# First attention beside the late projections, second beside the scan's second half and half of the output projection, with two w_in buffers

## What is computed

```python
proj = rmsnorm(x, norm1_g[l]) @ w_in[l]
pa, pb, pc, pd = jnp.split(proj, cut, axis=-1)
out_a = moba_attention(qa, ka, va, ...)      # attention "A", 4 heads of 64
out_b = rwkv7_time_mix(pb, ...)              # the scan, two channel halves c = 0, 1
out_c = sgu_mix(uc, vc, ...)                 # gated position mixing
out_d = diff_attention(qd, kd, vd, ...)      # attention "D", two softmaxes per head
mixed = jnp.concatenate([out_a, out_b, out_c, out_d], axis=-1)
x = x + mixed @ w_out[l]
x = x + hier_moe(rmsnorm(x, norm2_g[l]), ...)
```

## Time and profile before

| | us |
|---|---|
| median of 3 runs | 2249.1 |
| lowest and highest | 2246.83, 2253.64 |
| the profiled execution | 2240.36 |
| its span, first to last instruction | 2238.7 |

### The profile page before, as it was taken

One profiled execution on the slowest core, in us unless ns is written; L12 is line 12 of the kernel. 1 busy time (PEld: TensorE's weight loads), 2 busy tenths in 40 slices (PEclk: granted clock), 3 DMA queues, 4 the chain that ended last, 5 costly groups with the idle time before them and its releaser, 6 DMA issues. The chain is left out here.

```text
span 2238.7 us, 23731 instructions
## 1 busy us (share of the span) xinstructions
PE 1760.2 (79%) x9640; PEld 1014.2 (45%) x9640; DVE 583.6 (26%) x1175; ACT 328.0 (15%) x663; POOL 112.5 (5%) x133
## 2 busy tenths in 40 slices
PE   6799987698977768878379999777988877776862
PEld 3356574244544434444134656533544444443430
DVE  1262533543111111111124425334421111111113
ACT  1211233311000000000012121333100000000001
POOL 0010000001000000000100000000010000000001
PEclk9899996599998999889789999856999989998986
DMA  8911110025999999999541110100379999999993
GB/s 285 272 47 38 38 38 1 0 85 197 365 412 414 415 413 412 415 412 407 185 185 48 52 52 1 38 0 1 120 274 413 413 415 412 413 415 413 412 365 127
DMA packets 107426, 527.16 MB, mean 235 GB/s; under 512 B 35044, under 2 KB 35812, under 8 KB 88420
## 3 DMA queue, kind: packets, MB, share of 16 engines
q1 hardware_dynamic: 64740, 476.28, 52.6%
q0 software_dynamic: 38400, 33.79, 4.7%
q10 hardware_dynamic: 4224, 16.25, 3.0%
HBM read 482.03 MB, written 44.04 MB: 235 GB/s over the span
## 5 line engine op out<-in xcount | busy, mean ns | idle before, releaser
L747 PE MATMUL banks<-RING,TOK 128*64 128x256 f32 x4224 | 482.9, 384 | 75.4 <-DMA RING<-in_w_up 39.0
L747 PEld LDWEIGHTS banks<-RING,TOK 128*64 128x64 f32 x4224 | 322.0, 138 | 252.8 <-DMA RING<-in_w_up 52.6
L762 PE MATMUL banks<-RING,XS 128*64 128x512 f32 x1056 | 278.0, 673 | 39.7 <-issue 27.0
L463 PE MATMUL banks<-RING,XNT 128*128 128x512 f32 x512 | 238.5, 603 | 0.0
L762 PEld LDWEIGHTS banks<-RING,XS 128*64 128x64 f32 x1056 | 90.9, 156 | 187.8 <-issue 186.2
L1003 ACT ACTIVATE XS<-banks 128x256 f32<-128x256 f32 x64 | 24.6, 384 | 987.8 <-PE banks L747 987.8
L1374 DVE TENSOR_TENSOR XS<-XS,banks 128x256 f32<-128x256 f32 x66 | 27.8, 421 | 494.2 <-PE banks L747 494.2
L740 PE MATMUL banks<-CF,TOK 128*128 128x128 f32 (+1 forms) x272 | 53.5, 360 | 112.0 <-DMA TOK<-x_slots 109.9
L463 PEld LDWEIGHTS banks<-RING,XNT 128*128 128x128 f32 x512 | 92.2, 192 | 90.8 <-issue 90.4
L454 PE MATMUL banks<-XNT,RING 128*128 128x512 f32 x256 | 110.4, 593 | 2.8 <-DMA RING<-in_w_in_blocks 1.6
L1395 DVE COPY XS<-banks 128x512 f32<-128x512 f32 x64 | 44.3, 692 | 252.9 <-PE banks L762 252.9
(11 more groups left out here) (257 smaller groups left out, 1698.1 us busy)
## 6 DMA issues: line engine op xcount, KB each, us to landing
RING<-in_w_gate SPq DMA_DIRECT2D x66, 2048.0 KB, 27.3
RING<-in_w_up SPq DMA_DIRECT2D x66, 2048.0 KB, 28.1
RING<-in_w_down SPq DMA_DIRECT2D x66, 2048.0 KB, 25.3
RING<-in_w_in_blocks SPq DMA_DIRECT2D x12, 2048.0 KB, 11.7
TOK<-x_slots SPq DMA_DIRECT2D x32, 512.0 KB, 23.5
y_slots<-XS POOLq DMA_DIRECT2D x64, 256.0 KB, 19.2
x_slots<-TOK ACTq DMA_DIRECT2D x11, 1024.0 KB, 30.6
RING<-in_w_out_blocks SPq DMA_DIRECT2D x4, 2048.0 KB, 7.6
```

Source lines behind the costliest of these rows:

```text
L463: last = mm(bank[:, :], XNT[:, k, i * P:(i + 1) * P], w[:, k, :], start=(k == 0), stop=(k == KD - 1))
L747: last = mm(bank[f * CAP:(f + 1) * CAP, 0:256], XT[:, k, h * CAP:(h + 1) * CAP], w[:, k, f * 256:(f + 1) * 256], start=(k == 0), stop=(k = ...
L762: last = mm(PS[5][n * CAP:(n + 1) * CAP, :], HT[:, j, f * CAP:(f + 1) * CAP], w[:, k, n * BN:(n + 1) * BN], start=(k == 0), stop=(k == KF ...
```

## The change

- `SLOT` buffers for `w_in`: two instead of three, so that the third is free for A's and D's turned queries and keys (`QKT`) and probabilities (`PB`). The load of expert 0's gate weights moves from the end of the projections to the end of the mixers, since it goes to that buffer.
- The late projections share one PSUM bank (2) instead of two; the scan uses banks 1, 3 and 4.
- M and E steps are cut in two (q = 0, 1), so a scan half has 45 steps.
- All of scan half 0 and all of attention A are put beside the late projections; all of scan half 1 is put beside attention D, by the table `SCAN_PER_PART` (three scan steps behind each of D's first nine parts, two behind five, one behind eight).
- Half of the output projection (the inputs from A and from the gated mixer, k = 0, 1, 4, 5) is done during D in eight pieces of four matmuls (`out_half`), each added to X by VectorE in that order (`add_half`); the other half follows D.
- The gated mixer is done in two pieces, and group t(3,2) waits for the first, t(3,3) for the second; its two transposes (`turn_gated`) stand between the last projection and D.

```diff
+SCAN_PER_PART = [3] * 9 + [2] * 5 + [1] * 8
+SCAN_BANKS = (1, 3, 4)
...
-        QKT = view(XNTb, 0, 2048, "p (j t) -> p j t", j=4)
-        PB = view(XNTb, 2048, 2048, "p (b m t) -> p b m t", b=2, m=2)
         SLOT = [RING[:, s * 4096:(s + 1) * 4096] for s in range(6)]
+        QKT = view(RING, 2 * 4096, 2048, "p (j t) -> p j t", j=4)
+        PB = view(RING, 2 * 4096 + 2048, 2048, "p (b m t) -> p b m t", b=2, m=2)
...
-        MT = view(SC, 2048, 1024, "p (j t) -> p j t", j=2)
+        MT = view(XNTb, 0, 1024, "p (j t) -> p j t", j=2)
...
-        bank_of = [g % 8 if g < LATE else (0, 5)[g % 2] for g in range(len(PROJ))]
+        bank_of = [g % 8 if g < LATE else 2 for g in range(len(PROJ))]
...
-            steps = ([("P", q) for q in range(4)] + ["T"] + [(part, n) for n in range(1, 7) for part in "ME"]
+            steps = ([("P", q) for q in range(4)] + ["T"] + [(part, n, q) for n in range(1, 7) for q in range(2) for part in "ME"]
                      + [(part, ch) for ch in range(4) for part in "ZBS"] + [("F", n) for n in range(3)] + ["G"])
-            scan = [(c, m, step) for c, m in ((0, "A"), (1, "D")) for step in steps]
-            scan.remove((0, "A", "G"))
-            for g in range(LATE, len(PROJ)):
+            scan = {c: [(c, m, step) for step in steps] for c, m in ((0, "A"), (1, "D"))}
+            scan[0].remove((0, "A", "G"))
+            parts = {m: [(m, u, part) for u in range(PAIRS + n) for part in range(2)] for m, n in (("A", 2), ("D", 3))}
+
+            def late(g, quarter, steps):
+                yield "proj", (g, quarter)
+                for _ in range(steps):
+                    yield "rwkv", scan[0].pop(0)
+                if quarter == 3 and PROJ[g] == ("t", (2, NT - 1)):
+                    yield "sgu_in", ()
+                if quarter == 3 and PROJ[g] in (("t", (3, 1)), ("t", (3, 2))):
+                    yield "sgu_out", (PROJ[g][1][1] - 1,)
+
+            attended = PROJ.index(("t", (2, 0)))
+            for g in range(LATE, attended):
                 for quarter in range(4):
-                    yield "proj", (g, quarter)
-                    for _ in range(1 if g > LATE else (0, 0, 0, 4)[quarter]):
-                        yield "rwkv", scan.pop(0)
-                if PROJ[g] == ("t", (2, NT - 1)):
-                    yield "sgu_in", ()
-                if PROJ[g] == ("t", (3, 1)):
-                    yield "sgu_out", ()
-            for m, u in [("A", u) for u in range(PAIRS + 2)] + [("D", u) for u in range(PAIRS + 3)]:
-                yield "attn", (m, u, 0)
-                if scan:
-                    yield "rwkv", scan.pop(0)
-                else:
-                    yield "out", (u - PAIRS + 1,)
-                yield "attn", (m, u, 1)
-                if m == "A" and 1 <= u <= 4:
-                    yield "rwkv", scan.pop(0)
+                    yield from late(g, quarter, 1 if g > LATE else 0)
+            for n in range(4 * (len(PROJ) - attended)):
+                yield from late(attended + n // 4, n % 4, 2 if n % 8 == 7 else 1)
+                if n % 3 < 2 and parts["A"]:
+                    yield "attn", parts["A"].pop(0)
+            for t in range(2):
+                yield "sgu_turn", (t,)
+            for n, steps in enumerate(SCAN_PER_PART):
+                yield "attn", parts["D"].pop(0)
+                for _ in range(steps):
+                    yield "rwkv", scan[1].pop(0)
+                if n >= 6 and n % 2 == 0:
+                    yield "out", divmod((n - 6) // 2, NT)
+            assert not any(scan.values()) and not any(parts.values())
...
-                        if n >= 3:
-                            sp.wait_ge(proj_ps, BLOCK_USED[n - 3])
-                        sp.dma_start(SLOT[n % 3], w_in[one, n].rearrange("a p n -> p (a n)")).then_inc(slot_full[n % 3], 16)
+                        if n >= 2:
+                            sp.wait_ge(proj_ps, BLOCK_USED[n - 2])
+                        sp.dma_start(SLOT[n % 2], w_in[one, n].rearrange("a p n -> p (a n)")).then_inc(slot_full[n % 2], 16)
...
-                        sp.wait_ge(proj_ps, BLOCK_USED[n + 3])
+                        sp.wait_ge(proj_ps, BLOCK_USED[n + 4])
...
-                    load(0, 0, [(proj_ps, BLOCK_USED[5]), (mixed_done, 1), (mixed_done, 1)])
+                    load(0, 0, [(mixed_done, 1), (mixed_done, 1), (mixed_done, 1)])
...
+                            if PROJ[g] in (("t", (3, 2)), ("t", (3, 3))):
+                                pe.wait_ge(sgu_done, PROJ[g][1][1] - 1)
...
+                            _, n, q = step
+                            if n == 1:
+                                pe.wait_ge(s["turned"], 3)
+                                pe.wait_ge(s["eye"], 6)
+                            else:
+                                pe.wait_ge(s["de_merged"], 4 * (n - 2) + 2 * q + 2)
+                            if n > 1 or q:
+                                pe.wait_ge(s["m1_copied"], 2 * (n - 1) + q)
+                            for w in range(4):
+                                u = 4 * q + w
+                                last = mm(PS[1][:, w * P:(w + 1) * P], UB[:, u, 0:P], DB[:, u, :], start=True, stop=True)
+                            last.then_inc(s["m1_ps"], 1)
...
+                    def turn_gated(t):
+                        if t == 0:
+                            pe.wait_ge(sgu_done, 2)
+                            pe.wait_ge(proj_copied, len(PROJ) - 8)
+                        else:
+                            pe.wait_ge(mt_a, 1)
+                        for i in range(NT):
+                            last = tr(PS[2][:, i * P:(i + 1) * P], UV[:, i, t * P:(t + 1) * P], ident)
+                        last.then_inc(mt_ps, 1)
...
+                            pe.wait_ge(proj_copied, copied("t", (1, NT - 1)) if m == "A" else len(PROJ) - 8)
...
+                    def out_half(n, i):
+                        if n + i == 0:
+                            pe.wait_ge(mt_a, 2)
+                            pe.wait_ge(mix["A"]["o_done"], 2)
+                        else:
+                            pe.wait_ge(res_added, 4 * n + i)
                         if i == 0:
-                            pe.wait_ge(slot_full[0], 48)
-                            pe.wait_ge(mt_a, 2)
-                            pe.wait_ge(mix["D"]["y_done"], 1)
-                        project_out(0, i, range(KD - 2))
-
-                    run_mixers(proj=project, rwkv=rwkv, attn=attn, sgu_out=mix_positions, out=out_but_last)
+                            pe.wait_ge(slot_full[n], 64)
+                        project_out(n, i, (0, 1, 4, 5), 2).then_inc(res_ps, 1)
+
+                    run_mixers(proj=project, rwkv=rwkv, attn=attn, sgu_out=mix_positions, sgu_turn=turn_gated, out=out_half)
...
+                    pe.wait_ge(mix["D"]["y_done"], 1)
+                    pe.wait_ge(res_added, 8)
+                    for i in range(NT):
+                        project_out(0, i, (2, 3), OUT_BANK[i], last=False)
                     pe.wait_ge(sub_done, 2)
                     for i in range(NT):
-                        project_out(0, i, (KD - 2, KD - 1))
-                    pe.wait_ge(slot_full[1], 48)
+                        project_out(0, i, (6, 7), OUT_BANK[i], first=False).then_inc(res_ps, 1)
                     for i in range(NT):
-                        project_out(1, i, range(KD))
+                        project_out(1, i, (2, 3, 6, 7), OUT_BANK[NT + i]).then_inc(res_ps, 1)
...
+                    def add_half(n, i):
+                        dve.wait_ge(res_ps, 4 * n + i + 1)
+                        xv = X3[:, i, n * BN:(n + 1) * BN]
+                        V.tensor_tensor(xv, PS[2][:, :], xv, ALU.add).then_inc(res_added, 1)
+
+                    run_mixers(rwkv=rwkv, attn=attn, sgu_in=norm_v, sgu_out=gate_u, out=add_half)
```

More of the change, by code:

```diff
@@ new lines, in rwkv @@
+                            last.then_inc(s["m1_ps"], 1)
+                        elif step[0] == "E":
+                            _, n, q = step
+                            pe.wait_ge(s["m1_copied"], 2 * (n - 1) + q + 1)
+                            for side in range(2):
+                                if n == 6 and side == 0:
+                                    continue
+                                if n == 6:
+                                    pe.wait_ge(s["de_merged"], 20 + q)
+                                elif n > 1 or q > 0:
+                                    pe.wait_ge(s["de_merged"], 4 * (n - 1) + 2 * q + side - 1)
@@ L563, in rwkv @@
+                                    if side == 0:
+                                        last = mm(PS[3][:, w * P:(w + 1) * P], EB[:, u, :], MB[:, u, :], start=True, stop=True)
+                                    else:
+                                        last = mm(PS[4][:, w * P:(w + 1) * P], MB[:, u, :], EB[:, u, :], start=True, stop=True)
+                                last.then_inc(s["de_ps"], 1)
                         elif step[0] == "Z":
@@ L764, in down @@
```

(10 more changed lines are left out.)

142 lines of the change are left out of this document (51 added, 91 removed).

## The result

| | us |
|---|---|
| before, median | 2248.0 |
| changed, median of 4 runs | 2323.6 |
| lowest and highest of the changed kernel | 2319.4, 2329.4 |
| ratio, with its 95% interval | 1.034 (1.030 to 1.038) |
| profiled execution of the changed kernel, and its span | 2326.4, 2324.7 |

The change makes the kernel slower by 75.6 us. 2300 was predicted, with a range of 2238 to 2355. The two profiled executions stand 86.0 us apart, which is what the traces have to account for.

What follows compares the result with a forecast made beforehand. TensorE was taken to bound the late projections, with idle and clock loss elsewhere. Idle 92.3 plus clock 25 less 89.8 gave +27.5 us in layer 0, +29.2 in layer 1, less 5: 2249 + 52, rounded to 2300 us, range 2238 to 2355.

Steps and rivals of the forecast that it cites:

- turn beside the normalisation: Late projections: a turn of A's probabilities waits behind the gated mixer's normalisation on VectorE; 10.4 us idle per layer.
- other turns of A, first and second: Attention A: second heads' turns wait for ScalarE's copy, 5.0 us, first ones for VectorE, 5.0 us, per layer.
- small waits, and between the halves: Gated mixer's pieces, copies and A's first turns, 4.6 us; gated transposes, copies and D's rotation between halves, 4.5 us.
- P steps and T of half 1: Start of scan half 1: TensorE waits for VectorE's 13.3 us of work, little covering it; 8.5 us idle per layer.
- D's first turns: Attention D: eight first-head turns wait for probabilities behind VectorE's merges or additions, mean 2.2 us; 17.6 us per layer.
- M to E: Scan half 1: E waits for M's copy with nothing between, eight times 0.75 us plus 1.2; 7.2 us per layer.
- the end: End of the mixers: TensorE waits for D's second normalisation and half 1's finish; 16.8 us idle per layer.
- the clock: Clock 0.80 in D's stage, losing 21 us, plus 4 for other stalls; 25 us lost per layer.
- The turns' waits are hidden and the clock stays up: Rival in D: VectorE has the probabilities ready, saving first-turn waits and most related clock loss; 2229 us, chance 0.17.
- Only the clock stays up: Rival in D: the waits occur, but dense steps hold the upper clock level; 2258 us, chance 0.13.
- The lower level throughout: Rival in D: clock stays at 0.54 as before, 40 us more per layer; 2370 us, chance 0.12.
- A stall by a buffer or bank: Rival in the projections: a late w_in block stalls them; above 2300 us by its length, chance 0.02.

Runs made afterwards that it cites:

- experiment 1: Changed kernel, with VectorE normalising the probabilities of u - 1 right behind the maxima of u, ahead of the merges: 2246.1 us, ratio 1.000.
- experiment 8: Kernel before with only the probabilities ahead of the merges: 2206.8 us; changed kernel with three edits together 2229.8 us, with four edits 2214.3 us.
- experiment 7: Kernel before with only two w_in buffers, one PSUM bank for late projections and the later load of expert 0's gate weights: 2249.6 us, ratio 1.001.
- experiment 3: Changed kernel with two unused 128x512 matmuls before each of D's eight first turns: 2282.3 us, ratio 1.014.
- experiment 6: Changed kernel with the gated mixer's normalisation in four pieces: 2329.2 us; or kept whole, with A's parts moved away from it: 2328.8 us.
- experiment 5: Changed kernel with inputs k = 2 and 6 projected before the last wait: 2315.7 us; with norm2_g's load also ahead of expert 0's weights: 2303.1 us.

## Why the prediction came out as it did

The direction was right, the range held, and the largest mechanism is shown: experiment 1 takes away the first turns' waits and with them 77 us. It is not the only one: by the comparison in experiment 8, 39 us of the change's loss stay with that edit in both kernels, nearly all of it as idle time. The idle term, by its own steps, in layer 0:

| step of the prediction | priced | measured |
|---|---|---|
| turn beside the normalisation | 10.4 | 9.6 |
| other turns of A, first and second | 10.0 | 11.5 |
| small waits, and between the halves | 9.1 | 8.5 |
| P steps and T of half 1 | 8.5 | 5.0 |
| D's first turns | 17.6 | 17.1 |
| D's second turns | 5.0 | 4.9 |
| D's second scores | 4.9 | 4.1 |
| M to E | 7.2 | 6.2 |
| Z, B, S | 2.8 | 1.5 |
| the end | 16.8 | 14.8 |
| sum | 92.3 | 83.3 |

Each step is where it was said to be, and most are right to about 1 us. P and the end were over-priced, by 3.5 and 2.0, and A's turns under-priced by 1.5, since ScalarE's exponentials hold three of the second heads' turns for 1.2 to 1.5 us. P is less of a miss than it looks: the stretch in step with VectorE lasted 16.4 us (327.27 to 343.67) against 15.7 priced, but its clock was 0.58 on average, so TensorE's own products took 11.4 us and not 7.2. What is missing there as idle time is clock loss.

**The step that was mis-sized is the clock.** I took 0.80 in D and a loss of 25 us per layer, that is 13 less than before. The clock in D was 0.74 and 0.78, and the loss 52.0 and 39.1, more than before. Against the prediction that is +27 and +14, and the idle time is 9 less. Work that I took as unchanged was 3 to 4 us more per layer. Layer 0's mixers began 1.3 us earlier (2.3 in experiment 7), where 5 were taken back for the later third `w_in` block.

The miss has two halves. In D the loss was 35.5 and 28.3 us (136.72 x 0.26, 128.76 x 0.22), not 21. Part of that is a slip in the sum: it multiplies 105 us, which is near TensorE's work in D at full clock (136.72 x 0.74 = 101), by 0.20, but the loss is counted on the longer busy time; 105 us of work at 0.80 lose 105/0.80 - 105 = 26. Outside D the sum had 4 us; the runs show 16.5 and 10.8, most of it in the late projections with A (160.62 x 0.05 = 8 in layer 0), which were expected to run as before, and at the end of the mixers (17.49 x 0.24 = 4).

Why the clock in D was taken too high: I reasoned from the mean of A's stage before (0.82), with "a wait of about 3 us in front of each of eight turns, between denser stretches" (the idle sum has 2.2 for the same waits). The traces show that even 1.84 us before a turn, with shorter gaps near it, is followed by the lower level, and that this falls on the full matmuls of M and E behind the wait. The Trainium skill, "TensorE: Matmul & The Clock Gate", section "HAM oscillation — how this bites in real kernels", by which only long gaps would cost clock, was weighed and not followed; the trace disagrees with it in this kernel, at waits of 1.84 to 2.44 us, and experiment 3 shows that filling them gives the clock back.

**The rivals.** "The turns' waits are hidden and the clock stays up" did not hold for the change, since the probabilities did stand behind the merges, as the step said; but as a kernel it nearly exists, one edit away, at 2246 and clock 0.84 in D (2229 was worked out for it). "Only the clock stays up" fell with the clock at 0.74. "The lower level throughout" fell too. A stall by a buffer or bank is excluded by experiment 7 in the order of before, and in the changed kernel's mixers no wait of TensorE ends with a DMA.

**What stays open.** Idle time does not give the clock loss. Layers 0 and 1 of the changed kernel have 83.3 and 83.1 us of idle and lose 52.0 and 39.1 to the clock, and both edits of experiment 6 made idle time less and the kernel not faster. One execution of each kernel was profiled, so part of this may be spread from run to run. That the loss depends on where the waits fall in time is likely, and no run here isolates it. So what the normalisation costs by itself is not settled: its wait was removed twice and came back once as another, and its gain was smaller than the spread of the clock term. Nor is it settled how the 39 us that stay divide among the normalisation, P, M to E and the end; only for the end did edits give something back, 20.5 us in the two of experiment 5.

## What to carry to other kernels

Before moving work beside other work, look at the order of the engine that feeds TensorE. What decided half of it here was not how much VectorE had to do (26% of the span) but that it did a ready piece of work behind one that had only just become ready; doing the ready one first was worth 77 us in the changed kernel and 40 in the one before. And try such an edit in both kernels: the change cost 76 us as it stood and 39 with the order put right in both. Count a wait of TensorE of 2 us twice, once for its length and once for the clock behind it. When a wait goes, look for what is next in the same queue: a merge behind the normalisation, or a small DMA behind 6 MB of weights.

## What the runs showed of the hardware

- Two matmuls of 128x512 without a use, before each of D's eight first turns, made the changed kernel 41 us faster: clock in D 0.74 to 0.88.
- The lower level came behind waits of TensorE of only 1.8 to 2.4 us (clock 0.50 in the window 363 to 366, behind a wait of 1.84 and one of 0.46), behind 15 of the 16 first turns of D. It also came behind a single wait of 0.87 us at 371.31 in the changed kernel, and one of 0.92 at 371.45 in that of experiment 1.
- One program with the same idle time in both layers lost 52.0 us to the clock in one and 39.1 in the other.
- The 512 KB row issued behind three loads of 2 MB landed after 18.6 us; issued ahead of them it landed after 4.5 us, and the kernel was 12.6 us faster.
